# Hybrid decoder layer on one core: three of the four activation sums at the MLP's begin made by GpSimd instead of VectorE

## The reference, cut to what matters

```python
x = x + gate1 * rms_norm(y, g_post_mix[l])
h = rms_norm(x, g_pre_mlp[l]) * (1.0 + scale2) + shift2
u = jax.nn.relu(h @ w_mlp_up[l])          # 512 x 2048 @ 2048 x 8192
y = (u * u) @ w_mlp_down[l]
x = x + gate2 * rms_norm(y, g_post_mlp[l])
```

## Time and profile before

| | us |
|---|---|
| median of 3 runs | 2286.09 |
| lowest and highest of them | 2285.52, 2291.07 |
| the profiled execution, its own time | 2284.16 |
| its span in the trace | 2282.4 |
| PE busy | 2198.8 |
| VectorE busy | 1840.1 |
| ScalarE busy | 986.2 |
| GpSimd busy | 403.0 |

### The profile page before, as it was taken

How to read it: one execution, slowest core, us unless ns; L and a number is a source line. 1 busy time by engine, 2 the same in 40 slices (tenths; PEclk the granted TensorE clock), 3 DMA queues, 4 the chain that set the end, 5 groups by cost and what they waited for, 6 DMA issues and landing times.

```text
span 2282.4 us, 39170 instructions
## 1 busy us (share of the span) xinstructions
PE 2198.8 (96%) x15364; PEld 1975.2 (87%) x15364; DVE 1840.1 (81%) x2108; ACT 986.2 (43%) x1213; POOL 403.0 (18%) x278
## 2 busy tenths in 40 slices
PE   6899999999999999989999999999999999999996
PEld 2557687888777788789999999999999999999996
DVE  6849984997438684698999999999877878878788
ACT  4334425222347421555555555555533333333442
POOL 6540044444347000000000000000000112212120
PEclk8999999999999999999999999999999999999998
DMA  9887664335643397325655555666825636528334
GB/s 355 333 303 267 246 236 122 94 93 187 198 129 102 111 357 251 139 75 183 215 200 195 196 194 198 207 207 207 324 93 230 245 112 265 200 90 331 149 111 166
DMA packets 177008, 451.68 MB, mean 198 GB/s; under 512 B 17648, under 2 KB 73072, under 8 KB 164720
## 3 DMA queue, kind: packets, MB, share of 16 engines
q1 hardware_dynamic: 117104, 385.93, 47.3%
q10 hardware_dynamic: 59776, 63.97, 8.3%
HBM read 377.75 MB, written 71.84 MB: 197 GB/s over the span
## 4 chain that ended last, share of the span: by engine, by line
PE 52%; DVE 3%; issue 1%; ACT 1%; DMA 1%; DVEq 0%; ACTq 0%
PE psum L1046 17%; PE psum L1045 17%; PE psum L1047 17%; DMA u2f<-f_lo 1%; DVE w_lo L2466 0%; DVE B_raw L2738 0%; DVE T_parts L2722 0%; DVE x_odd L2618 0%; DVE f_lo L2511 0%; DVE w_lo L2524 0%; ACT w_hi L1783 0%; DVE y_half L2584 0%; DVE y_half L2606 0%; DVE y_half L2596 0%; DVE raw L2618 0%
## 5 line engine op out<-in xcount | busy, mean ns | idle before, releaser
L1023 POOL TENSOR_TENSOR y_half<-y_half,part 128x512 f32<-128x512 f32 x44 | 87.3, 1995 | 1379.3 <-DVE y_half L2629 1379.3
L1045 PE MATMUL psum<-T_parts,w_hi 128*128 128x256 f32 x1024 | 288.9, 282 | 10.6 <-DVE u_t L2755 5.2
L1046 PE MATMUL psum<-w_lo,T_parts 128*128 128x256 f32 x1024 | 289.8, 283 | 0.0
L1047 PE MATMUL psum<-w_hi,T_parts 128*128 128x256 f32 x1024 | 289.3, 282 | 0.0
L1047 PE MATMUL psum<-T_parts,w_lo 128*128 128x256 f32 x1024 | 288.1, 281 | 0.0
L1046 PE MATMUL psum<-T_parts,w_hi 128*128 128x256 f32 x1024 | 288.1, 281 | 0.0
L1045 PE MATMUL psum<-w_hi,T_parts 128*128 128x256 f32 x1024 | 287.1, 280 | 0.2 <-DVE w_lo L2524 0.2
L1495 ACT ACTIVATE w_hi<-raw 128x1024 fp32r<-128x1024 f32 (+1 forms) x128 | 129.1, 1016 | 334.3 <-PE psum L1047 270.8
L974 POOL TENSOR_TENSOR w_lo<-raw,w_hi 128x1024 fp32r<-128x1024 f32 (+1 forms) x80 | 194.4, 2439 | 365.3 <-ACT w_hi L1495 365.3
L1045 PE MATMUL psum<-h_hi,w_hi 128*128 128x512 f32 (+1 forms) x592 | 238.6, 403 | 8.7 <-issue 4.4
L1046 PE MATMUL psum<-h_lo,w_hi 128*128 128x512 f32 (+1 forms) x592 | 236.3, 399 | 0.0
(11 more groups left out here) (364 smaller groups left out, 5647.2 us busy)
## 6 DMA issues: line engine op xcount, KB each, us to landing
raw<-in_w_in SPq DMA_DIRECT2D x88, 512.0 KB, 5.7
mod_ring<-in_w_mod_first SPq DMA_DIRECT2D x32, 1024.0 KB, 9.5
mod_slab<-in_w_mod SPq DMA_DIRECT2D x32, 1024.0 KB, 5.3
raw<-in_w_up_units SPq DMA_DIRECT2D x64, 512.0 KB, 5.2
unit_odd<-in_w_up_units SPq DMA_DIRECT2D x64, 512.0 KB, 5.6
raw<-in_w_down_units SPq DMA_DIRECT2D x64, 512.0 KB, 5.3
unit_odd<-in_w_down_units SPq DMA_DIRECT2D x64, 512.0 KB, 5.4
T_parts<-u2f SPq DMA_DIRECT2D x28, 1024.0 KB, 13.5
```

The source lines that it names most:

```text
L1023: nc.gpsimd.tensor_tensor(y, y, part[:], ALU.add).then_inc(y_pool, 1)
L1045: nc.tensor.matmul(o, a_hi, b_hi, start=first, stop=False)
L1046: nc.tensor.matmul(o, a_hi, b_lo, start=False, stop=False)
L1047: return nc.tensor.matmul(o, a_lo, b_hi, start=False, stop=last)
```

## The change

The sums T3, T2 and T4 leave VectorE's list and are put at GpSimd's, behind attention's last squares and ahead of the MLP's second matmul, in the same two halves each. T1 stays on VectorE as `first_t_sum`. The buffers, the forms and the counts of `t_ready` are the same. GpSimd waits for the fourth group of `h_full_of` (by halves), for T1's or B21's low part where the sum is written in its place, and for the sum before.

```diff
@@ gpsimd, behind squares_of @@
+            def t_sum(name):
+
+                q = h2_quad
+                to, a, b, low_of = {"T3": (q["T3"], q["B22"], q["B12"], 2), "T2": (q["T2"], q["B22"], q["T1"], 6),
+                                    "T4": (q["T4"], q["B21"], q["T2"], 4)}[name]
+                for hf in range(2):
+                    pool.wait_ge(h_full_ready, 3 * HALF + HALF // 2 * (hf + 1))
+                    pool.wait_ge(b_lo_ready, low_of)
+                    pool.wait_ge(t_ready, 2 * T_SUMS.index(name))
+                    nc.gpsimd.tensor_tensor(to[:, quarter(hf), :], a[:, quarter(hf), :], b[:, quarter(hf), :],
+                                            ALU.subtract).then_inc(t_ready, 1)
+
+            for name in T_SUMS[1:]:
+                t_sum(name)
@@ vector, the MLP's begin @@
-            t_sum("T1")
+            first_t_sum()
             b_low(2)
             after_start(0)
             after_start(1)
...
             after_start(4)
-            t_sum("T3")
             b_low(4)
             after_start(5)
-            t_sum("T2")
             after_start(6)
             b_low(5)
             after_start(7)
-            t_sum("T4")
             b_low(6)
```

More of the change, by code:

```diff
@@ L479, in wait_quads, with quarter @@
                 eng.wait_ge(odd_landed, i * (QUADS * 16 * BLOCK // 2) + QUADS * 16 * (n // 2 + 1))
+        def quarter(hf):
+            return slice(HALF // 2 * hf, HALF // 2 * hf + HALF // 2)
         def dn_unit(n, kb):
@@ L2713, in _ @@
             x1_scales(TT - 1, TT)
-            def quarter(hf):
-                return slice(HALF // 2 * hf, HALF // 2 * hf + HALF // 2)
             def b_low(m):
@@ L2723, in b_low, with first_t_sum @@
                                     b_hi[name][:, quarter(hf), :].bitcast(F32), ALU.subtract).then_inc(b_lo_ready, 1)
[L2725 to L2729, removed]
-                for hf in range(2):
[L2731 to L2738, removed]
+            def first_t_sum():
+                for hf in range(2):
+                    dve.wait_ge(h_full_ready, 2 * HALF + HALF // 2 * (hf + 1))
+                    dve.wait_ge(b_lo_ready, 2)
+                    V.tensor_tensor(h2_quad["T1"][:, quarter(hf), :], h2_quad["B12"][:, quarter(hf), :],
+                                    h2_quad["B11"][:, quarter(hf), :], ALU.subtract).then_inc(t_ready, 1)
             def comb(n, m, i):
```

## The result

| | before | after |
|---|---|---|
| median of 12 runs each, same series | 2287.09 us | 2294.16 us |
| lowest and highest of them | 2283.75, 2292.18 | 2284.63, 2297.88 |
| ratio after to before, 95% interval | | 1.0025 (1.0014 to 1.0036) |
| the profiled execution, its own time | 2284.16 us | 2297.88 us |

The account below looks back on a forecast made before the run. VectorE was taken to bound the MLP's begin, a chain carrying its delay to the end: +13.20 - 0.15 - 0.33 - 6.84 - 1.21 - 0.27 = +4.4 us on 2286.09 gives 2290.5, range 2286.5 to 2294.

Parts of the forecast that it names:

- the chain over the store: From VectorE's instruction at 1016.64 through unit 0's forms and their store: carries any delay to PE's start and the end.
- The rival by which the chain does not carry it all: Store or a load behind 1016.64 has slack, so only PE's own shift counts: +2.4 us, 2288.5; chance 0.16.
- turns of 2.26: Two-operand SBUF instructions on VectorE and GpSimd run one at a time; each GpSimd sum holds VectorE up 2.26 us.
- 12.7 net for six: VectorE's loss beside GpSimd's six half sums: 2.20 us each, 13.20 together, less 0.15 and 0.33 hidden.
- u3: VectorE instruction (`u_t`) that frees the bank for product (0,6); forecast to end at 1015.8 instead of 1011.33.
- The alternative of a hold as long as the whole undisturbed instruction: The Trainium skill's exclusive lock on VectorE beside GpSimd: each hold 2.40 us, sum +5.2, or 2291.3.
- 6.84 + 1.21 + 0.27: VectorE's savings: six instructions at 1.14 us, the pause ahead of T4's low part, and the pause at 1016.64.
- +4.4: Net delay in us forecast at VectorE's 1016.64, and so at PE's start and the program's end; chance 0.68.
- The store: Store of unit 0's forms, behind the low part at 1034.56, on which ScalarE's next forms depend: 11.51 us.
- Free running on both engines: No turn-taking at the MLP's begin: sums done at 996.1, VectorE's row 8.3 us shorter, 2277.8; chance 0.05.
- Dearer holds: Same turn-taking, but a turn costs 2.67 us or more, bringing the sum over 6.9; chance 0.11.
- the fall: PE's clock drop after its long wait, 1.2 GHz in place of 2.4, forecast to come at 992.4 and cost nothing.

Follow-up runs that it names:

- six subtractions more: Kernel before, all sums on VectorE, plus six 128x1024 subtractions on GpSimd whose results nobody reads: median 2302.61 us, ratio 1.0058.
- no sums: Changed kernel with the three sums left out, GpSimd only waiting and counting the semaphore up: median 2280.19 us, ratio 0.9960.
- T4 early: Kernel before with T4's sum moved ahead of T2's low part in VectorE's row, nothing on GpSimd: median 2290.01 us, ratio 0.9999.
- memsets: Changed kernel with each of GpSimd's six half sums replaced by a memset of the same 128x1024 piece: median 2282.57 us, ratio 0.9971.

## Why the prediction was right, step by step

**What bounds.** VectorE's row up to the comb of (0,6), then the chain over the store, carried to the end. Shown: across kernels from 28.3 to 49.1 in the comb column, the column of PE's start follows it at a distance of 36.1 to 37.4, and the rest up to the end of the span falls into the two groups of the pace. Behind 1080 PE waits for nothing in the first profile of the changed kernel; its third has one wait of 1.0 us, at 1080.3, and with six subtractions more there were two, 1.8 us together. The rival by which the chain does not carry it all (+2.4) falls.

**What is added.** Predicted: turns of 2.26, 3.34 a pair, 2.20 lost per sum, 12.7 net for six. Measured 12.58 (changed kernel against no sums), and, from the end of the first to the end of the last of VectorE's six long instructions 988.95 to 1005.50, 3.31 a pair, so a turn of 2.23. The numbers by the clock held as well: u3 was predicted to end at 1015.8 and ended at 1018.91 - 3.23 = 1015.68, GpSimd to be done at 1001.3, and it was at 1004.42 - 3.23 = 1001.19. The alternative of a hold as long as the whole undisturbed instruction (2.40) would have made a pair 3.48 and the sum +5.2, where +4.0 was measured.

**What is removed.** Predicted 6.84 + 1.21 + 0.27 = 8.32, measured 8.57. With both terms off by 0.1 and 0.2 the net came out at +4.0 instead of +4.4 in the comb column (+3.7 against the other two profiles before).

**What was missing.** The store. The prediction left it at 11.51 us, a term that it did not expect to move. In the four profiles of the changed kernel it took 12.4 to 12.6, which carries PE's start to +4.9 for the first pair, +4.7 between the means (78.1 and 73.4). It also took 12.7 with only T3 moved and once with T4 early, and 11.4 to 11.9 in the other eight, those with six GpSimd subtractions included. It shares the DMA engines with the four quarter loads, whose issues begin 2.2 us before its own in both kernels (1034.84 and 1037.04 before, 1042.07 and 1044.27 after). Why it was late four times of four in the changed kernel is open; chance is not excluded.

**The rivals.** Free running on both engines (-8.3, 2277.8) was the trap in this change: GpSimd idle, VectorE the bound, sums that nobody wants yet. It is what memsets do, at 28.29. Dearer holds (over +6.9) did not happen. The account of the chip ahead of the prediction has the engines wait for one another only through semaphores; the rows here show one wait more, a turn between VectorE and GpSimd that no semaphore asks for, and which stands in the trace as a longer instruction and not as idle time.

**The clock.** As predicted the fall moved to the wait ahead of (0,3), 0.55 us for the matmul behind 7.29 us of idle. The granted clock was 0.54 from 996 to 1000 and 1.00 after that, so that the first matmul of (0,6) took 0.35 us where it had taken 0.55 before. That this was worth nothing is read from the chain, which passes through VectorE there, and was not tried by itself.

**The size in the time.** By the ratios, +5.7 and +3.7 us in two series of runs (by the medians +7.1 and +4.7), around a predicted 4.4 and a +4.7 in the traces. The two engines' part of this was predicted to within 0.4 to 0.7 us. That the time came as near as it did is partly luck, since the store was left out of the sum, and start of the fourth group (978.2 to 984.2), store (11.4 to 12.7) and pace (6 us) scatter by 6, 1.3 and 6 us between executions. No cause of theirs is known, and none of it is shown to come from the change.

## What to carry to other kernels

An idle GpSimd is no free place for work taken from a busy VectorE. If VectorE's instructions there read two operands from SBUF, GpSimd's reading takes turns with them, and each 128x1024 subtraction on GpSimd costs VectorE 2.2 us to save it 1.14. Before moving one, look in the same trace for a place where both engines work at once, and price the move by the durations there. By the rows here, work that only writes can go to GpSimd, and reading work can go where VectorE reads PSUM (its `comb` kept 0.41 us beside a sum) or idles. What a VectorE instruction with a single operand from SBUF does beside such work was not tried.

Before reading a difference of two profiles as the change's, take distances from an event just ahead of the change, and profile each kernel more than once: here some 9 of 13.7 us (3.2 ahead of the change and 5.5 of pace) are seen between executions of one kernel too.

## What had not been expected of the hardware

The pace of PE in the MLP's first loop has two values, 3411 or 3412 matmuls in 400 us and 3373 or 3374, with the granted clock at 1.00 and PE busy for all of the 400 us. That is 117.2 and 118.6 ns for a matmul (the expectations above have 117.8 and 119.1 for the same two), and about 6 us over the loop. Both occurred with the kernel before and both with T4's sum early, from one execution to another. In the second matmul of the MLP all executions agreed, with 4169 matmuls from 1700 to 2200. Nothing in the traces says what sets it.

A copy of 128x1024 float32 on GpSimd took 1.5 to 1.9 us beside VectorE, with a turn of 0.91, against 2.26 for a subtraction: by that pair of rows a second operand costs GpSimd 1.35 us more, not the same again.
